# Modulation blocks issued in halves between turns, part of them among the convolved projections; latent values with the values stationary

## The reference

```python
mod_l = jnp.split((silu_c @ ada_w[l] + ada_b[l])[:, None, :], N_MOD, axis=-1)
mod_c = jnp.split(silu_cc @ ada_w[l] + ada_b[l], N_MOD, axis=-1)
h_l = modulate(rmsnorm(x, norm_mix_pre[l]), mod_l[0], mod_l[1])
...
ssd_c, diff_c, mla_c = jnp.split(h_ctx @ w_in, cuts, axis=-1)
...
s = jnp.einsum('bqhd,bkhd->bhqk', q, k).astype(F32) * scale
p = jax.nn.softmax(s, axis=-1)
return jnp.einsum('bhqk,bkhd->bqhd', p.astype(v.dtype), v)
...
out_l = jnp.concatenate([s_l, d_l, a_l], axis=-1) @ w_out
```

## Time and profile before

| | |
|---|---|
| time, median of 3 runs | 2326.37 us (2323.27 to 2326.76) |
| the profiled execution | 2327.59 us, its span 2325.5 us |
| busy: PE, DVE, ACT, POOL | 2030.5 us (87%), 596.4 us (26%), 525.7 us (23%), 211.1 us (9%) |
| mean granted clock of PE | 0.935 |
| latents to attention, layer 0 and 1 | 260.29 to 301.56, 1447.49 to 1482.73 |
| latent attention, layer 0 and 1 | 301.56 to 370.88, 1482.73 to 1537.61 |
| third modulation part, layer 0 and 1 | 370.88 to 386.74, 1537.61 to 1555.08 |

### The profile page before, as it was taken

The page is one execution under the profiler, slowest core; times in us unless marked ns, Lnnn a source line. Parts: engine busy times, 40 slices in busy tenths (PEclk is TensorE's granted clock), DMA queues, the critical chain, the costliest instruction groups (busy, mean ns, idle before and its releaser), DMA issues.

```text
span 2325.5 us, 25409 instructions
## 1 busy us (share of the span) xinstructions
PE 2030.5 (87%) x10730; PEld 1022.7 (44%) x10730; DVE 596.4 (26%) x1107; ACT 525.7 (23%) x1023; POOL 211.1 (9%) x225
## 2 busy tenths in 40 slices
PE   4988999998959999999997999999885887777775
PEld 2666565644423333333334776666443222222222
DVE  2156142254241111101104173322433100000002
ACT  4154342343210000000005162432422000000002
POOL 0400000020010111111111000000200100000000
PEclk9999999999969999999997999999987898988998
DMA  9510403202068999999998100432015999999997
GB/s 335 149 37 1 181 1 127 73 1 95 32 226 316 395 395 395 402 395 394 395 388 287 45 28 29 153 127 73 37 46 197 361 401 401 406 401 401 402 401 267
DMA packets 166370, 534.53 MB, mean 230 GB/s; under 512 B 10600, under 2 KB 19122, under 8 KB 166258
## 3 DMA queue, kind: packets, MB, share of 16 engines
q1 hardware_dynamic: 148112, 487.39, 53.8%
q0 software_dynamic: 16480, 40.21, 6.2%
q10 hardware_dynamic: 1666, 5.31, 0.6%
HBM read 507.72 MB, written 25.17 MB: 229 GB/s over the span
## 4 chain that ended last, share of the span: by engine, by line
PE 70%; DMA 11%; DVE 7%; SPq 6%; ACT 4%; issue 2%; ACTq 0%; DVEq 0%; POOL 0%; POOLq 0%
PE ps L2293 15%; PE ps L1777 9%; PE ps L2221 6%; PE ps L2347 6%; SPq L605 6%; PE ps L2302 5%; PE ps L1809 5%; PE ps L1786 5%; PE ps L1820 3%; DMA mod_rows<-in_w_up 3%; PE ps L1794 3%; DMA arena<-in_w_up 3%; PE ps L2356 2%; PE ps L2116 2%; DMA ring<-in_w_up 2%
## 5 line engine op out<-in xcount | busy, mean ns | idle before, releaser
L2293 PE MATMUL ps<-ring,arena 128*64 128x512 f32 x1056 | 249.3, 625 | 45.5 <-DMA ring<-in_w_up 30.2
L2293 PE MATMUL ps<-arena 128*64 128x512 f32 x892 | 216.0, 634 | 30.4 <-DMA arena<-in_w_up 30.4
L1777 PE MATMUL ps<-arena,ring 128*128 128x256 f32 (+1 forms) x640 | 203.6, 481 | 8.9 <-ACT arena L802 5.9
L2293 PEld LDWEIGHTS ps<-ring,arena 128*64 128x64 f32 x1056 | 80.8, 144 | 202.7 <-issue 202.7
L1777 PEld LDWEIGHTS ps<-arena,ring 128*128 128x128 f32 x640 | 123.0, 193 | 88.2 <-issue 69.8
L1809 PE MATMUL ps<-arena 128*128 128x256 f32 (+3 forms) x432 | 152.8, 488 | 7.9 <-ACT arena L848 4.4
L2293 PEld LDWEIGHTS ps<-arena 128*64 128x64 f32 x892 | 70.0, 146 | 166.3 <-issue 166.3
L2221 PE MATMUL ps<-ring,arena 128*128 128x512 f32 x320 | 139.6, 594 | 0.9 <-DVE arena L1584 0.9
L1698 DVE TENSOR_TENSOR arena<-arena,ps 128x512 f32<-128x512 f32 x32 | 22.0, 688 | 452.7 <-ACT arena L1128 452.7
...
L848 ACT ACTIVATE arena<-ps,nmax 128x768 f32<-128x768 f32 (+1 forms) x120 | 97.2, 813 | 133.0 <-DVE nmax L1226 122.0
L2347 PE MATMUL ps<-ring,arena 128*64 128x512 f32 x544 | 122.6, 594 | 0.7 <-ACT arena L1142 0.7
...
## 6 DMA issues: line engine op xcount, KB each, us to landing
...
```

The source lines that it names most:

```text
L1777: ins = mm(o[0:n, c0:c1], w[:, k, col:col + n], hT[:, k, c0:c1], start=k == 0, stop=k == KD - 1)
L2293: ins = mm(ps[0][hf * 64:hf * 64 + 64, col:col + 512], xl[e % 2][:, at:at + CAP_L], w[c][:, hf * 512:hf * 512 + 512], start=b + c == 0, st ...
```

## The change

**Latent attention.** Units now go in pairs of heads on the same query tile (`pair_jobs`), scores run two units ahead, and there are three buffers of exponentials and four of turned ones. In the value products the values are stationary (64 columns) and the turned probabilities move (128 columns); the two heads of a pair write partitions 0 to 63 and 64 to 127 of one slot. The result comes out turned, so DVE scales the exponentials themselves before they are turned (a pass over 128x768), and one DVE copy per pair puts the result into `mlaT`. The output projection reads `mlaT` directly: six blocks are turned and scaled instead of eight.

**Modulation.** Part 1 is issued in halves of four products with turns and column products between them, the turns of latents 0 lie in the last projection of the latents, and the columns of blocks 2 and 3 in the query products. Part 2 lies among the convolved projections: rows between them, single column products inside them, the last block after `cum` and in `z0`. Slots and the order of the weight loads follow: the weights of the first four projections are loaded ahead of part 2's blocks. In layer 0, part 0's blocks 2 and 3 lie between the turns of the tokens.

```diff
-                        ("matt", 3 * MH * q),
-                        ("ada2", 4), ("xbc", CONV_T), ("cum", 1), ("acT", 2), ("z0", 1), ("xT", NT),
+                        ("matt", 5 * MH // 2 * q),
+                        ("xbc", CONV_T + 3), ("cum", 1), ("ada11", 1), ("acT", 2), ("z0", 1), ("xT", NT),
...
+def pair_jobs(n):
+
+
+    order = [("score", 0), ("score", 1)]
+    for u in range(2 * n):
+        order += [("score", u + 2)] * (u + 2 < 2 * n) + [("turn", u)]
+        order += [("value", u // 2 - 1)] * (u >= 2 and u % 2 == 0)
+    order.append(("value", n - 1))
+    return {job: i for i, job in enumerate(order)}
...
-        return JOBS[l, "pre"] + (0, 3, 5, 6)[b]
-    return JOBS[l, f"ada{part}"] + b + (NT if l == 0 and part == 0 and b >= 2 else 0)
+        return JOBS[l, "pre"] + (1, 3, 4, 6)[b]
+    if part == 2:
+        return JOBS[l, "xbc"] + (1, 3, 7)[b] if b < 3 else JOBS[l, "ada11"]
+    return JOBS[l, "ada0"] + (b if l else (0, 1, 5, 8)[b])
...
+    return (b, 7 + b, (12, 13, 15, 16)[b])[part]
...
+    return JOBS[l, "xbc"] + (0, 2, 4, 5, 6, 8)[m]
...
-    return JOBS[l, "pre"] + (1, 2, 4)[i]
+    return JOBS[l, "pre"] + (0, 2, 5)[i]
...
-    return JOBS[0, "h"] - 2 + t
+    return JOBS[0, "ada0"] + (2, 3, 4, 6, 7, 9)[t]
...
+        matt = view(ar(a0, NT * 256), t=NT)
+        mlaT = view(ar(a0 + NT * 256, 2 * TOK), k=2)
...
+        PM = [ar(a3 + i * TOK, TOK) for i in range(3)]
+        PT_m = [ar(a3 + (3 + i) * TOK, TOK) for i in range(4)]
...
-                srcs += [aw[:, :, b * BLK:(b + 1) * BLK] for b in range(4, 12)]
-                srcs += [wi[:, :, c:c + n] for c, n in ((COL_X, 512), (COL_B, 256), (COL_Z, 512))]
+                srcs += [aw[:, :, b * BLK:(b + 1) * BLK] for b in range(4, 8)]
+                srcs += [wi[:, :, COL_X:COL_X + 512]]
+                srcs += [aw[:, :, b * BLK:(b + 1) * BLK] for b in range(8, 10)]
+                srcs += [wi[:, :, COL_B:COL_B + 256]]
+                srcs += [aw[:, :, b * BLK:(b + 1) * BLK] for b in range(10, 12)]
+                srcs += [wi[:, :, COL_Z:COL_Z + 512]]
...
-                rows_out(0, 0, 2)
+                    if t == 4:
+                        rows_out(0, 0, 2)
...
+                turned_latents(0)
                 rows_out(l, 1, 0)
                 latent_norms(2)
-                turned_latents(0)
                 turned_latents(1)
+                columns_out(l, 1, 0)
                 rows_out(l, 1, 1)
-                columns_out(l, 1, 0)
                 turned_latents(2)
+                rows_out(l, 1, 2)
                 columns_out(l, 1, 1)
-                rows_out(l, 1, 2)
                 rows_out(l, 1, 3)
+                columns_out(l, 1, 2)
...
+                columns_out(l, 1, 3)
                 heads_out(QT, jb("mq") + 1, 0, tq, MQK ** -0.5)
-                columns_out(l, 1, 2)
-                columns_out(l, 1, 3)
...
-                modulation(l, 2)
...
+                    j = conv_job(l, m)
...
+                    block = {0: 0, 1: 1, 4: 2}.get(m)
+                    if block is not None:
+                        rows_out(l, 2, block)
+                    act.wait_ge(*J.freed(j))
+                    act.activation(XB[:, m, :], XB[:, m, :], ACT.Silu).then_inc(S["xbc_ready"], 1)
+                    if block is not None:
+                        columns_out(l, 2, block)
+                rows_out(l, 2, 3)
...
+                columns_out(l, 2, 3)
...
+                def probabilities(u):
+
+                    nk, c = n_keys(q[u // 2 % nq]), u % 3
+                    dve.wait_ge(*J.freed(pair("score", u)))
+                    dve.reciprocal(rcol[:, c:c + 1], esum[:, c:c + 1]).then_inc(dve_step, 1)
+                    dve.wait_ge(*v.next(dve_step))
+                    dve.tensor_scalar(PM[c][:, 0:nk], PM[c][:, 0:nk], rcol[:, c:c + 1], None, ALU.mult)\
+                        .then_inc(S["prob_ready"], 1)
...
+                def pair_out(i):
+
+                    j, t = pair("value", i), q[i % nq]
+                    dve.wait_ge(*J.filled(j))
+                    dve.tensor_copy(mlaT[:, i // nq, t * P:(t + 1) * P], J.tile(j)[:, 0:P]).then_inc(*J.free(j))
+
+                maximum(0)
+                maximum(1)
+                for u in range(2 * np_ + 3):
+                    if u < 2 * np_:
+                        probabilities(u)
+                    if u + 2 < 2 * np_:
+                        maximum(u + 2)
+                    if u >= 3 and u % 2:
+                        pair_out(u // 2 - 1)
...
-                        TT(mixT[i % 2], view(J.tile(j)[:, :], k=KD),
-                           fac[:, 0:8].unsqueeze(2).to_broadcast([P, KD, P]), ALU.mult).then_inc(*J.free(j))
+                        TT(mixT[i % 2][:, 0:6, :], view(J.tile(j)[:, 0:6 * P], k=6),
+                           fac[:, 0:6].unsqueeze(2).to_broadcast([P, 6, P]), ALU.mult).then_inc(*J.free(j))
...
+                            ins.then_inc(*J.fill(j))
+                        if columns_of is not None and c1 == 512 and k >= 4:
+                            block_column(*columns_of, k - 4)
...
+                if not first:
+                    pe.wait_ge(*J.empty(j))
+                    arrived(n)
+                for k in range(KD) if first is None else range(first, first + 4):
+                    r = 32 * (k % 4)
+                    ins = mm(J.tile(j)[r:r + 32, 0:BLK], view(sc[:, :], k=KD)[:, k, :], ringv(n)[:, k, :], start=k < 4,
+                             stop=k >= 4)
+                if first != 0:
+                    ins.then_inc(half_used, 1)
...
+                if c == 0:
+                    pe.wait_ge(*w_.next(S["mod_rows"]))
+                ins = mm(J.tile(j)[:, BLK + 2 * c:BLK + 2 * c + 2], mrow[b % 2][:, c * P:(c + 1) * P],
+                         kc(K_TWO, 2), start=True, stop=True)
+                if c == 3:
+                    ins.then_inc(*J.fill(j))
...
                 for t in range(NT):
                     pe.wait_ge(*w_.next(S["xn_ready"]))
+                    if t == NT - 1:
+                        block_columns(0, 0, 2)
                     turn_tile(turn_job(t), lambda k: Fa[:, t, k * P:(k + 1) * P])
-                block_rows(0, 0, 0, 2)
-                block_rows(0, 0, 0, 3)
-                block_columns(0, 0, 2)
+                    if t in (2, 4):
+                        block_rows(0, 0, t // 2 + 1)
                 block_columns(0, 0, 3)
...
+                j = jb("mla") + 2
+                pe.wait_ge(*J.empty(j))
+                for b in range(2):
+                    t = 4 + b
+                    for k in range(KD):
+                        ins = mm(J.tile(j)[:, b * 512:b * 512 + MLA_COLS + 16], hT[:, k, t * P:(t + 1) * P],
+                                 w[:, k, 0:MLA_COLS + 16], start=k == 0, stop=k == KD - 1)
+                        if b and k == KD - 1:
+                            ins.then_inc(*J.fill(j))
+                        if b:
+                            turned_latent(0, k)
+                for k in (0, 4):
+                    block_rows(l, 1, 0, k)
+                    for n in range(k, k + 4):
+                        turned_latent(1, n)
+                for k in (0, 4):
+                    block_rows(l, 1, 1, k)
+                    for c in (k // 2, k // 2 + 1):
+                        block_column(l, 1, 0, c)
+                for k in (0, 4):
+                    block_rows(l, 1, 2, k)
+                for n in range(8):
+                    turned_latent(2, n)
+                block_rows(l, 1, 3, 0)
                 block_columns(l, 1, 1)
-                block_rows(l, 1, wb + 7, 2)
-                block_rows(l, 1, wb + 7, 3)
...
+                def pair_values(i):
+
+                    n, j = n_keys(q[i % nq]) // P, pair("value", i)
+                    for u in (2 * i, 2 * i + 1):
+                        pe.wait_ge(*J.freed(pair("turn", u)))
+                    pe.wait_ge(*J.empty(j))
+                    for k in range(n):
+                        for b in range(2):
+                            h = 2 * (i // nq) + b
+                            ins = mm(J.tile(j)[64 * b:64 * b + 64, 0:P], VM[:, k, h * MV:(h + 1) * MV],
+                                     PT_m[(2 * i + b) % 4][:, k * P:(k + 1) * P], start=k == 0, stop=k == n - 1)
+                    ins.then_inc(*J.fill(j))
...
+                w = arrived(wb + 11)
+                feature_major(conv_job(l, 0), w, 0, P)
+                block_rows(l, 2, 0)
+                feature_major(conv_job(l, 1), w, P, P, columns_of=(l, 2, 0))
+                block_rows(l, 2, 1)
+                feature_major(conv_job(l, 2), w, 2 * P, P, columns_of=(l, 2, 1))
+                feature_major(conv_job(l, 3), w, 3 * P, P)
+                w = arrived(wb + 14)
+                feature_major(conv_job(l, 4), w, 0, P)
+                block_rows(l, 2, 2)
+                feature_major(conv_job(l, 5), w, P, P, columns_of=(l, 2, 2))
...
+                block_rows(l, 2, 3)
...
```

(6 more changed lines are left out.)

203 lines of the change are left out of this document (105 added, 98 removed).

## The result

The changed kernel takes **2287.31 us** (median of 4 runs, 2286.11 to 2289.16); the kernel before, 2326.57 (2323.27 to 2328.64). The ratio is 0.9833, 95% interval [0.9816, 0.985]: 39 us less. The forecast was 2288, range 2277 to 2308. One of the twelve runs of experiment 4, 2519.77 us at a granted clock of 0.814, belongs to a slower state and is left out of its range and ratio. The profiled execution took 2287.51 us, its span 2285.5 against 2325.5 before.

A forecast was written before the change was run, and what follows sets the result against it. PE's own work was taken as the bound (70% of the chain of waits), some of it at 1.2 GHz. 14 + 11.4 + 12.1 - 1 + 2 = 38.5 us off 2327.6 gives 2289.1; stated 2288 us, range 2277 to 2308.

The forecast's parts named there:

- Value products, -14: Latent attention: value records 56 ns instead of 107, PE waiting 0.37 us per pair for DVE's scaling; 14 us less.
- Rival B: Latent attention: strips of 64 columns do not work side by side; 2308 us, or 2328 with loads in line; chance 0.07.
- Rival D: Latent attention: the clock falls and stays down, at 1.2 GHz 85 us more, 2370 us; chance 0.04.
- E: Latent attention: DVE's passes, slow form and long hand-overs eat the values' gain; 6 to 14 us back, 2299; chance 0.08.
- Third part, -11.4: Third modulation part among convolved projections: waits of 3.09 us covered and lost clock regained, no discount for columns; 11.4 us less.
- rival C: Among the projections: a slot or transfer becomes late; up to 3 us per layer, 2294 us; chance 0.08.
- Latents, -12.1: Latents and part 1: two waits of 0.81 us go, three quarters of 14.0 us lost clock return; 12.1 us less.
- rival A: Latents and part 1: turns and columns still let the clock fall, most of 10.5 us not won; 2297 us; chance 0.18.
- Start of layer 0, +1: Start of layer 0: last tile's turn, columns and copies in one line, 1.5 us longer, block 3's rows earlier; 1 us more.
- Output projection, -2: Output projection: two fewer turns per tile and a shorter first scaling by DVE; 2 us less.

The follow-up runs named there:

- experiment 4: Kernel before with only the latent attention in pairs and shorter output turns; start, latents and third part in the old order: 2308.32 us, ratio 0.994.
- 7: Changed kernel with a pair's value products one head behind the other, instead of changing strips at each product: 2304.8 us, ratio 0.9917.
- experiment 2: Changed kernel with the third modulation part as a run of its own ahead of the convolved projections again: 2302.31 us, ratio 0.9918.
- experiment 5: Changed kernel with column products of part 1's blocks 2 and 3 as one run of eight between the two query products: 2306.29 us, ratio 0.9927.
- experiment 6: Changed kernel with the latents' turns and rows in whole runs again, new slots and columns inside the queries kept: 2287.77 us, ratio 0.9847.
- experiment 3: Changed kernel with latents and first modulation part in the old order, turns, rows and columns in whole runs, old slot numbering: 2294.9 us, ratio 0.9897.
- experiment 1: Changed kernel with the start of layer 0 in its old order, blocks 2 and 3 behind the sixth turned tile: 2286.88 us, ratio 0.9857.

## Why the prediction was right, and where it was not

The time (2287.3 for 2288) and the mechanisms of the three large terms were right. By its steps:

1. **Value products, -14: right.** 8.0 and 5.8 measured in the trace, and 4 and 7 show that they come from the pairs and from the strips. Some 1.5 of the 8.0 are clock, though: the old attention of layer 0 ran 3 us at 0.50 near its start (0.98 over all), the new one at 1.00 throughout, and the forecast had nothing for that. Inside, two errors cancel: 61 ns a record for 56 (0.12 a pair), and PE waits 0.14 for the scaling, with 0.14 ahead of the values, for the single wait of 0.37. Rival B was near on its price, 107 ns for one strip at a time (99.6), and wrong on its premise. Rival D did not come: clock 1.00 in both attentions. Nor did E: DVE's slow form was not taken, 0.62 a pass.
2. **Third part, -11.4: right, slightly high.** By the traces 4.4 and 6.0, 10.4; by experiment 2, 9.9. The waits of 3.09 and the clock are its two halves, the columns got no discount, and no slot or transfer came late (rival C): PE is busy 70.86 of 70.86. The 1.0 that is missing is the 24 column products inside projections, 0.045 us dearer each. The forecast's 0.98 a block was itself the length of the records with their drain; by starts it was 0.90. Whether the wait for ACT or the runs of columns let the clock fall there was not tried apart.
3. **Latents, -12.1: right in sum, partly for another reason.** 14.6 less 1.8 for the moved turns is 12.8. The granted clock came back whole, to 1.00, and not by three quarters, so rival A fell. But full clock and both waits would have given 15.6: the wait ahead of the attention grew by 0.27 in each layer, which the forecast had unchanged, and the rest of the difference was not taken apart. The forecast named runs of column products; experiment 5 shows that one such run alone lowers the clock. It also gave weight to turns beside columns; experiment 6 shows none. And 14.0 us of lost clock was one execution's figure: experiment 3 shows 13 in its profile's stages and 8 in its median, waits included.
4. **Start of layer 0, +1: the step that failed.** The trace says -3.6, the order itself +0.3 (experiment 1). "Turn, columns and copy stand in one line" was right, 9.2 us for 9.3. Counted from the first turn, that chain is 1.3 us longer (forecast 1.5) and block 3's rows end 1.04 earlier: the forecast took some of that away for "rows at the lower clock", but a block's rows took 1.85 us there, as fast as the 1.8 behind the turns. And the forecast set its sum against a profile whose own start was late, 54.93 where every other trace has 48.8 to 51.6, without a second trace to say so.
5. **Output projection, -2: 1.4.** From router to experts 138.45 became 137.59 in layer 0, and the end of layer 1 is 0.6 shorter.

What made the sum so close is in part luck. Against the forecast's 38.5 the two traces differ by 40.0: the start is 4.6 better, which the change did not do, and the latents 0.8; the third part is 1.0 worse, the output projection 0.5, the attention 0.2, and stretches for which the forecast had nothing are 2.1 longer.
